# The last tile of a norm fed in two halves, in a two-block transformer kernel on one core

## The reference

```python
def rms_norm(x, gain):
    xf = x.astype(jnp.float32)
    y = xf * lax.rsqrt(jnp.mean(xf * xf, axis=-1, keepdims=True) + EPS)
    return (y * gain.astype(jnp.float32)).astype(x.dtype)

# first model, for each of 2 layers
x = x + 0.5 * swiglu_ffn(rms_norm(x, ffn1_norm[l]), ffn1_w_in[l], ffn1_w_out[l])
h = rms_norm(x, mix_norm[l])
...                                     # three branches out of h, merged
x = x + merged @ w_out[l]
x = x + 0.5 * swiglu_ffn(rms_norm(x, ffn2_norm[l]), ffn2_w_in[l], ffn2_w_out[l])

# second model, for each of 2 layers, on latent (and context) rows
h = gated_residual(h, ml, 0, swiglu(ada_in(h, norm_g[i, 0], ml, 0), ...), 0.5)
h = gated_residual(h, ml, 1, yl, 1.0)   # yl: retention in layer 0, neighbourhood attention in layer 1
h = gated_residual(h, ml, 2, swiglu(ada_in(h, norm_g[i, 2], ml, 2), ...), 0.5)
...
return rms_norm_2(h, final_norm_g)
```

## Time and profile before

| | us |
|---|---|
| median of 3 runs | 3204.93 |
| lowest, highest | 3204.53, 3206.68 |
| the profiled execution | 3203.71 |
| its span, first to last instruction | 3201.8 |
| PE busy | 3140.3 (98%) |
| DVE busy | 1992.3 (62%) |
| ACT busy | 1357.8 (42%) |

### The profile page before, as it was taken

The page is one execution under the profiler, slowest core; times in us unless marked ns, Lnnn a source line. Parts: engine busy times, 40 slices in busy tenths (PEclk is TensorE's granted clock), DMA queues, the critical chain, the costliest instruction groups (busy, mean ns, idle before and its releaser), DMA issues.

```text
span 3201.8 us, 39778 instructions
## 1 busy us (share of the span) xinstructions
PE 3140.3 (98%) x15550; PEld 2619.4 (82%) x15550; DVE 1992.3 (62%) x2797; ACT 1357.8 (42%) x1907; POOL 129.9 (4%) x160
## 2 busy tenths in 40 slices
PE   8999999999999999999999999999999999999998
PEld 7888888888888887888878888788887788887787
DVE  7968778788687787663344444776335643345665
ACT  6546655455566555323233333322223322245553
POOL 1000000000000000000000000300000000021000
PEclk9999999999999999999999999999999999999999
DMA  8765356677554576542332222254324633253354
GB/s 252 250 193 178 127 197 224 223 236 242 157 184 132 197 246 207 188 147 93 105 99 80 79 93 86 99 171 156 108 92 158 212 117 105 93 139 92 106 189 153
DMA packets 334901, 496.78 MB, mean 155 GB/s; under 512 B 11042, under 2 KB 221884, under 8 KB 334716
## 3 DMA queue, kind: packets, MB, share of 16 engines
q1 hardware_dynamic: 330652, 483.46, 45.5%
q0 software_dynamic: 4064, 10.77, 1.6%
HBM read 493.09 MB, written 1.10 MB: 154 GB/s over the span
## 4 chain that ended last, share of the span: by engine, by line
PE 94%; DVE 3%; issue 1%; ACT 1%; DMA 0%; POOL 0%; SPq 0%; DVEq 0%; POOLq 0%; ACTq 0%
PE bank L587 24%; PE bank L589 23%; PE bank L588 23%; PE bank L643 13%; PE bank L647 7%; PE bank L602 1%; DVE wlo L1750 0%; PE bank L788 0%; PE bank L773 0%; PE bank L1067 0%; DMA raw<-in_w_in_dram 0%; DVE bank L2592 0%; POOL small L2660 0%; PE bank L610 0%; ACT npr L1698 0%
## 5 line engine op out<-in xcount | busy, mean ns | idle before, releaser
L1750 DVE TENSOR_TENSOR wlo<-raw,whi 128x1024 fp32r<-128x1024 f32 (+1 forms) x780 | 939.6, 1213 | 893.7 <-ACT whi L1231 891.6
L1231 ACT ACTIVATE whi<-raw 128x1024 fp32r<-128x1024 f32 (+1 forms) x780 | 815.9, 1050 | 1150.3 <-PE bank L589 990.3
L587 PE MATMUL bank<-xTh,whi 128*128 128x512 f32 (+1 forms) x1312 | 508.2, 387 | 7.2 <-DVE xTl L1835 7.2
L589 PE MATMUL bank<-xTh,wlo 128*128 128x512 f32 (+1 forms) x1312 | 504.0, 384 | 0.0
L588 PE MATMUL bank<-xTl,whi 128*128 128x512 f32 (+1 forms) x1312 | 503.7, 384 | 0.0
L643 PE MATMUL bank<-xT,whi 128*128 128x512 f32 x1760 | 441.5, 393 | 0.9 <-DVE xT L1835 0.5
L587 PE MATMUL bank<-whi,hh 128*128 128x512 f32 x968 | 377.9, 390 | 0.0
L589 PE MATMUL bank<-whi,hl 128*128 128x512 f32 x968 | 376.8, 389 | 0.0
L588 PE MATMUL bank<-wlo,hh 128*128 128x512 f32 x968 | 376.6, 389 | 0.0
L643 PEld LDWEIGHTS bank<-xT,whi 128*128 128x128 f32 x1760 | 316.5, 189 | 63.0 <-issue 3.4
L587 PEld LDWEIGHTS bank<-xTh,whi 128*128 128x128 f32 x1312 | 246.6, 188 | 66.9 <-issue 16.3
(11 more groups left out here) (383 smaller groups left out, 3651.9 us busy)
## 6 DMA issues: line engine op xcount, KB each, us to landing
raw<-in_ffn_w_in_dram SPq DMA_DIRECT2D x176, 1024.0 KB, 5.2
raw<-in_ffn_w_out_dram SPq DMA_DIRECT2D x80, 1024.0 KB, 5.1
mraw<-in_w_mod_dram SPq DMA_DIRECT2D x72, 1024.0 KB, 5.1
raw<-in_w_in_dram SPq DMA_DIRECT2D x44, 1024.0 KB, 5.2
raw<-in_ret_w_in_dram SPq DMA_DIRECT2D x24, 1024.0 KB, 5.1
raw<-in_w_branch_dram SPq DMA_DIRECT2D x12, 1024.0 KB, 5.0
raw<-in_nat_w_qkv_dram SPq DMA_DIRECT2D x12, 1024.0 KB, 5.2
raw<-in_ffn_w_out_dram SPq DMA_DIRECT2D x16, 512.0 KB, 3.4
```

Source lines behind the costliest of these rows:

```text
L587: pe.matmul(ps, lh, rh, start=start, stop=False, skip_group_check=True)
L589: return pe.matmul(ps, ll, rh, start=False, stop=stop, skip_group_check=True)
L1231: nc.scalar.activation(hi, src, ACT.Copy).then_inc(*e.inc("hi", key, part))
L1750: nc.vector.tensor_tensor(lo, src, hi.bitcast(F32), ALU.subtract).then_inc(*e.inc("lo", key, part))
```

## The change

There are five parts.

1. At eleven seams (all but (`f1`, 0) and (`g2`, 1)) the last tile's last slabs are computed 256 columns at a time: first columns 0 to 255 of the half into the tile's bank, then columns 256 to 511 into another bank, `rest` (`rows_by_tile`). Where the bank already holds the sums of earlier slabs, DVE adds those of columns 256 to 511 to X as a piece of its own (`begun`). So X's last half comes as pieces `first`, `begun` and `rest`; behind retention as `first` and `rest`.
2. The tile before the last is scaled between these pieces (`after_first`). ACT squares only the first piece; DVE adds its sum (`mean_begun`), and then one DVE operation over the 256 columns of `rest`, which starts from that sum, gives the mean square that POOL reads.
3. Behind retention (`g2`, 0) ACT squares all tiles, not only the odd ones, and a tile's factor is asked for one tile later.
4. The transposes: before the last tile all others are transposed, at every seam but the first; the second four column blocks take their banks one at a time; the ring of banks is turned so that the bank of `rest` comes last. At (`g2`, 1) ACT alone scales tile 0.
5. With 512 rows DVE makes the first slab's second `wlo` in two operations, the first of them ahead of the last tile's scaling (`low_begun`). In feed-forward blocks with 256 rows both banks of a pair are freed by DVE's sum.

```diff
+def halved(name):
+    return name not in (("f1", 0), ("g2", 1))
+def squared_on_act(name, t):
+    return t % 2 == 1 or name == ("g2", 0)
+def pieces_of_rows(name, t, n, whole=False):
+    if n == 0 or t != last_tile(name) or not halved(name):
+        return [Piece(n)]
+    first = Piece(n, ("first",), (), 0, 256, True, whole)
+    begun = [] if whole else [Piece(n, ("begun",), (), 256, 256, False, True, True)]
+    return [first, *begun, Piece(n, ("rest",), ("rest",), 0, 256, after_first=whole)]
...
@@ PE, rows_by_tile
+                    if halved and t == tiles[-1]:
+                        columns(t, ps[t][:, 0:256], slice(0, 256), ("first",), k0, 0, False)
+                        rest = new(*name, t, "rest", ring=REST_OF[ring])
+                        columns(t, rest[:, 0:256], slice(256, 512), ("rest",), k0, k0, True)
+                    else:
+                        columns(t, ps[t][:, :], slice(0, 512), (), k0, 0, t == tiles[-1])
...
@@ PE, turn_in
-                    groups = (order[:-1], order[-1:]) if name in BEHIND_DOWN else (order,)
+                    groups = (order,) if name == ("f1", 0) else (order[:-1], order[-1:])
...
@@ DVE
+            def mean_begun(name, t):
+                dve.wait_ge(*e.at("ssa", name, t, 1))
+                link(STT(small[:, t:t + 1], small[:, t:t + 1], EPS, small[:, 4 + t:5 + t], ALU.add, ALU.add))
             def mean_square(name, t):
-                if t % 2:
+                if halved(name) and t == last_tile(name):
+                    dve.wait_ge(*e.at("X", name, t, 1, "rest"))
+                    a = X[:, t, 768:1024]
+                    V.tensor_tensor_reduce(junk_v[:, 0:256], a, a, 1.0 / D, small[:, t:t + 1], ALU.mult, ALU.add,
+                                           small[:, 12 + t:13 + t]).then_inc(*e.inc("ms", name, t))
+                    return
...
+                rows(last, 1, after_first, lambda: mean_begun(name, last))
+                mean_square(name, last)
+                if late:
+                    scaled(before)
+                if T == 512:
+                    low_begun(FIRST[name], 1)
+                scaled(last)
```

More of the change, by code:

```diff
@@ L722, in rows_by, with rows_by_tile, columns @@
                 return k0
[L724 to L731, removed]
+            def rows_by_tile(keys, name, ps, xh, xl, k0, total, ring="all", ahead_of_tile=lambda t: None, halved=False):
+                def columns(t, dst, c, key_of, k, clears, uses):
                     for key in keys:
@@ L1033, in mixers @@
                 wo = {}
+                L.units["short"] = 0
                 for n in range(2):
@@ L1796, in scaled @@
                 def scaled(t):
-                    if t % 2 and (name, t) != (("g1", 0), 3):
-                        mean_square(name, t)
+                    if all(engine == "act" for engine, _, _ in scaled_by(name, t)):
+                        return
                     dve.wait_ge(*e.at("rstd", name, t))
@@ L1803, in scaled @@
                                 .then_inc(*e.inc("xn", name, t, i))
-                order, scales = tile_order(name, T), []
-                for t in order:
+                order = tile_order(name, T)
+                if name == ("f1", 0):
+                    squares(name, 0, 1)
+                    mean_square(name, 0)
+                    scaled(0)
+                    mean_square(name, 1)
+                    scaled(1)
+                    columns(0)
+                    until(0)
+                    dve.wait_ge(*e.at("cols_copied", 0))
+                    return
@@ L1807, in norm @@
+                late = name == ("g2", 0)
+                for i, t in enumerate(order[:-1]):
                     if name == ("g1", 0) and t == 2:
                         dve.wait_ge(*e.at("used", (("f2", 1), "down", 1, 3), 1))
-                    if scales and name in BEHIND_DOWN:
-                        scaled(scales.pop())
-                    if rows and t < tiles:
+                    if late:
+                        if i >= 2:
+                            scaled(order[i - 2])
                         rows(t)
-                    if t % 2 == 0 and t < tiles:
-                        squares(name, t, 1)
-                        mean_square(name, t)
@@ new lines, in norm, with after_first @@
+                    if t < tiles:
+                        rows(t)
+                        if not squared_on_act(name, t):
+                            squares(name, t, 1)
+                            mean_square(name, t)
+                last, before = order[-1], order[-2]
+                def after_first():
+                    if late:
+                        mean_square(name, before)
+                    else:
+                        scaled(before)
+                if late:
+                    scaled(order[-3])
```

230 lines of the change are left out of this document (145 added, 85 removed).

## The result

| | before | changed |
|---|---|---|
| median of 6 runs each | 3205.8 us | 3216.6 us |
| lowest, highest | 3204.29, 3209.25 | 3214.72, 3220.41 |
| span of the profiled execution | 3201.8 | 3212.9 |

The ratio is 1.0033 with a 95% interval of 1.0023 to 1.0043: 0.33% slower, where the forecast was 3202.3 and its range ended at 3206.5. Of all rivals none had this mechanism.

What follows compares the result with a forecast made beforehand. PE, busy 98% of the span, was taken as the bound, with 23.8 us of waits at the seams. Terms 1.5 + 2.4 + 0.2 - 1.7 + 0.2 = 2.6 us took 3204.9 to 3202.3; range for 8 in 10, 3197.0 to 3206.5.

Steps and rivals of the forecast that it cites:

- the banks' new order and the freeing of pairs by DVE's sum cost nothing: Banks at the seams: 5.5 us each for two PE steps between uses of a pair's bank, so no cost.
- The fourth rival: Pieces don't come apart: PE waits for the bank of `rest`, or transposes for theirs; 3205 to 3208, chance 0.04.
- Three seams with 256 rows behind a feed-forward block: At (`mx`, 0), (`f1`, 1), (`mx`, 1) the last tile's scaling starts 0.50 us earlier each, gain 1.5.
- Three with a gate: At (`r`,), (`g1`, 1), (`n`,), 512 rows, DVE the limit: scaling 0.53 us earlier, gain 0.63 each.
- `last`: The last seam, with 512 rows and a gate, where the output follows: gain 0.53 us.
- (`g1`, 0): 512 rows without a gate: scaling 0.5 us earlier, but 24 transposes stand ahead of the last tile's; gain 0.2.
- (`f2`, l): Two seams behind the merge: DVE arrives late and every piece queues on it; loss 0.84 us each, 1.7 together.
- (`g2`, 0): Behind retention: gain 2.0 us at full clock, 0.2 at the slow clock, which the forecast took.
- (`g2`, 1): Tile 1's chain as it was, its squares perhaps queued behind a scaling on ACT: 0, at most 0.5 us lost.
- the clock did stay up at retention: Rival: shorter gaps keep PE at 2.4 GHz behind retention and at (`mx`, 1); 3198 to 3200.5, chance 0.20.
- the second: Rival: clock falls at more seams, as the gap at (`f2`, l) grows to 5.3 us; 3203 to 3206, chance 0.12.
- DVE late at every seam: Rival: `rest` queues on DVE behind scaling, `begun` and `mean_begun`; 3213 if all seams go like (`f2`, l), chance 0.06.

Runs made afterwards that it cites:

- the first experiment: The changed kernel without the line that restarts the ring of short banks ahead of `wo`: 3202.59 us, ratio 0.9993 to the kernel before.
- the third: The changed kernel without the restart ahead of `wo`, its ring of short banks begun at bank 2 in each mixer: 3204.62 us, ratio 0.9995.
- e4_f2_whole: The fourth experiment: the third with the last tile computed, added and squared whole again at (`f2`, 0) and (`f2`, 1): 3204.75 us, ratio 0.9994.
- e7_f2_g21_whole: `e4_f2_whole` with (`g2`, 1) as before, DVE and ACT scaling tile 0 together and ACT squaring first: 3204.25 us, ratio 0.9993.
- e9_down_whole_b: The third with the last tile whole at eight seams, all but (`f2`, l) and retention, and no split `wlo` at the whole seams: 3210.47 us, ratio 1.0010.
- e12_no_low_begun: The third without the split of the first slab's second `wlo`, made whole behind the last tile's scaling: 3204.76 us, ratio 0.9996.

## Why the prediction was wrong, step by step

**The step that failed** is "the banks' new order and the freeing of pairs by DVE's sum cost nothing". It held for the pairs and for `rest`, which were looked at, as far as PE's waits show: the one new long wait for a bank is for `short`. It wasn't asked of `short`, whose start the change also sets, and whose price was 12 to 14 us: 4.55 us of waiting for DVE in each layer, and a slow clock behind each wait. The fourth rival had a wait for a bank, but as a wait for `rest` or of the transposes, at 3205 to 3208. Without the restart the time is 3202.59, and the forecast was 3202.3. That the two agree is in part luck: the first experiment's interval reaches 1.0001, so no gain over the kernel before is shown by it, the third has 3204.62, and the terms erred both ways. At the full clock behind retention, which they got, the prediction's terms add up to 4.4 us; as measured in the profiles they are 1.8:

- *Three seams with 256 rows behind a feed-forward block*, 0.50 each: 0.38. `rest` is taken 0.38 behind the last matmul's start (0.32 assumed) and reaches scaling in 1.61 (1.56).
- *Three with a gate*, 0.63 each: 0.12. The order on DVE was right to 0.02: `rest` starts at 1653.83, 2.36 behind tile 2's sum, where 2.38 was forecast. But from there to scaling it takes 2.46 and not 2.02, and POOL's 0.93 in place of 0.55 is the most of it; the rest is the squares, 0.48 and 0.08 for 0.44. The Trainium skill ("GPSIMD Engine Reference", section Specifications) says that POOL shares its SBUF interface with DVE and contends with DVE instructions that have two SBUF inputs. This trace agrees: the `wlo` has two, and 0.55 became 0.93. The rows of the changed kernel, the first beside the 1636.67 of the earlier trace rows:

```profile
1651.47 0.16 DVE L1861 SCALAR_TENSOR_TENSOR small<-small 128x1 f32<-128x1 f32 x1
...
1653.83 0.42 DVE L2127 TENSOR_TENSOR sg<-bank,gb 128x256 f32<-128x256 f32 x1
```

- *`last`*, 0.53: 0.49.
- *(`g1`, 0)*, a gain of 0.2: 0.05.
- *(`f2`, l)*, a loss of 0.84 each: 0.7 and 1.1 by the third and fourth experiments. DVE goes from piece to piece as written. Beside the earlier trace rows, of the changed kernel:

```profile
455.65 0.42 DVE L2531 TENSOR_TENSOR X<-bank,X 128x256 f32<-128x256 f32 x1
456.40 0.49 DVE L1883 TENSOR_SCALAR xn<-X,small 128x512 f32<-128x512 f32 x1 [0.33 <-POOL small L2786]
456.80 0.42 DVE L2531 TENSOR_TENSOR X<-bank,X 128x256 f32<-128x256 f32 x1
457.14 0.15 DVE L1850 SCALAR_TENSOR_TENSOR small<-small 128x1 f32<-128x1 f32 x1
457.36 0.42 DVE L2531 TENSOR_TENSOR X<-bank,X 128x256 f32<-128x256 f32 x1
...
458.98 0.88 DVE L1883 TENSOR_SCALAR xn<-X,small 128x256 f32<-128x256 f32 x3 [0.67 <-POOL small L2786]
```

- *(`g2`, 0)*, 0.2 at the slow clock and 2.0 at the full one: 1.66, since the clock stayed at 1.00. It did so in the changed kernel and six experiments, and fell in `e4_f2_whole`, `e7_f2_g21_whole`, `e9_down_whole_b` and `e12_no_low_begun`, with gaps of 9.8 to 10.1. Scaling of tile 3 came 4.2 us behind PE's end, where 4.1 was forecast. Beside the earlier trace rows:

```profile
2070.55 1.04 PE L814 MATMUL bank<-cst,xn 128*128 128x128 f32 x8
2074.31 2.84 PE L814 MATMUL bank<-cst,xn 128*128 128x128 f32 x24 [2.72 <-DVE xn L1883]
2078.83 0.47 PE L616 MATMUL bank<-xTh,whi 128*128 128x512 f32 x1 [1.69 <-DVE xTl L1945]
```

- *(`g2`, 1)*, 0: a loss of 0.14.

Of the rivals, the clock did stay up at retention, and it fell at (`f2`, l) as the second had it; both happened in one kernel. DVE late at every seam did not happen: it idles 1.00 ahead of `rest` at (`f1`, 1). Of the three signs by which the prediction would be wrong, the clock came true: it was 1.00 in both windows. PE's waits for `xn` fell to 13.5 us in 12, where they were to stay near 16. The wait that decided the time was on no list.

## What to carry to other kernels

Where banks are handed out by a counter, a line that sets the counter moves no instruction and adds no work, and yet decides for which reader each next block waits. For each such line, list which bank the next block gets, who read it last and when that read ends, and hold this against the moment at which PE wants it; on the engine that reads late, the work that stands ahead of its read (here two `wlo`) is part of the price. And the idle time of an engine is not free to fill when the engine that it waits for is slowed down by the filling: here DVE waited for POOL, and DVE's `wlo` made POOL slower.

## What the hardware showed that was not expected

- POOL's power on one column takes 0.55 us, and 0.93 with a `wlo` of 512 columns on DVE beside it (at (`g1`, 0), (`r`,), (`g1`, 1), (`n`,)), 0.72 at (`g2`, 0), and 0.55 again at the first four when that `wlo` is gone.
- A wait of PE of 4.55 us between two blocks at full clock cost 6.4 to 6.7 us against the third experiment's same stretch (249.63 against 243.20, 247.92 against 241.25).
- The same gap can be followed by either clock: at (`f1`, 1) a gap of 4.70 had 1.00 behind it in the kernel before, and 0.79 in 646 to 654 in `e9_down_whole_b`. What decides is open.
- What a fall costs depends on what PE waits for while it lasts: up to 1.7 us in a stream of matmuls, 0.1 behind (`n`,).
